# Four of the first 16 modulation pieces scaled by ScalarE and summed by TensorE, and the bias rows behind two loads

## The reference

```python
c_act = jax.nn.silu(c)
for l in range(DEPTH):
    mod = (c_act @ w_ada[l] + b_ada[l])[:, None, :]          # 1024 x 6144 weights
    sh_a, sc_a, g_a, sh_m, sc_m, g_m = jnp.split(mod, 6, axis=-1)
    h = x * (1.0 + sc_a) + sh_a
    proj = h @ w_in[l]
    ...      # three attention mixers, output projection w_o, layer norm
    ...      # second modulation, squared-ReLU MLP of width 4096, layer norm
```

## Time and profile before

| | us |
|---|---|
| median of 3 runs (lowest to highest) | 1343.76 (1343.13 to 1343.97) |
| the profiled execution, its own time | 1341.76 |
| its span (first to last instruction) | 1340.0 |
| TensorE busy in it | 1299.1 |
| VectorE busy in it | 972.2 |
| ScalarE busy in it | 603.3 |

### The profile page before, as it was taken

The page is one execution under the profiler, slowest core; times in us unless marked ns, Lnnn a source line. Parts: engine busy times, 40 slices in busy tenths (PEclk is TensorE's granted clock), DMA queues, the critical chain, the costliest instruction groups (busy, mean ns, idle before and its releaser), DMA issues.

```text
span 1340.0 us, 19979 instructions
## 1 busy us (share of the span) xinstructions
PE 1299.1 (97%) x6888; PEld 1106.5 (83%) x6888; DVE 972.2 (73%) x1646; ACT 603.3 (45%) x1244; POOL 317.2 (24%) x428
## 2 busy tenths in 40 slices
PE   7998999999999999999999999999999999999996
PEld 5897797988878888888879977888897888888885
DVE  6779898867787867876674668997679456544678
ACT  4465889824323222212255668995263222221321
POOL 0041376603010110010030506774130010001005
PEclk9999999999999999999999999999999999999998
DMA  9774100142644664462224330010335333323322
GB/s 360 282 233 143 57 1 28 64 154 68 234 159 158 224 206 146 172 225 88 85 69 151 113 122 1 15 46 24 118 124 181 97 95 97 100 94 95 101 94 102
DMA packets 89217, 165.09 MB, mean 123 GB/s; under 512 B 8435, under 2 KB 19059, under 8 KB 89132
## 3 DMA queue, kind: packets, MB, share of 16 engines
q1 hardware_dynamic: 88980, 163.71, 36.7%
q10 hardware_dynamic: 152, 0.28, 0.1%
HBM read 161.84 MB, written 4.21 MB: 124 GB/s over the span
## 4 chain that ended last, share of the span: by engine, by line
PE 77%; DVE 12%; ACT 5%; DMA 3%; POOL 1%; issue 1%; SPq 0%; DVEq 0%; ACTq 0%
PE bank L1790 23%; PE bank L1792 22%; PE bank L1791 22%; PE bank L2070 4%; DVE ada_sum L1091 2%; DMA ada_b<-in_b_ada 1%; PE bank L2054 1%; PE bank L1729 1%; DMA slab_raw<-in_w 1%; DVE stats L1453 1%; DVE sqr L1436 1%; PE bank L2046 1%; PE bank L2045 1%; DVE ada_sum L1118 1%; DVE h_lo L1540 1%
## 5 line engine op out<-in xcount | busy, mean ns | idle before, releaser
L1790 PE MATMUL bank<-hT_hi,slab_hi 128*128 128x512 f32 (+1 forms) x640 | 236.6, 370 | 3.0 <-DVE qC L1306 3.0
L1792 PE MATMUL bank<-hT_hi,slab_lo 128*128 128x512 f32 (+1 forms) x640 | 235.4, 368 | 0.0
L1791 PE MATMUL bank<-hT_lo,slab_hi 128*128 128x512 f32 (+1 forms) x640 | 235.4, 368 | 0.0
L1532 DVE TENSOR_TENSOR slab_lo<-slab_raw,slab_hi 128x512 fp32r<-128x512 f32 x240 | 166.7, 741 | 86.8 <-ACT slab_hi L1035 64.6
L1790 PE MATMUL bank<-slab_hi,h_hi 128*128 128x512 f32 x512 | 200.5, 392 | 1.9 <-DVE slab_lo L1532 1.9
L1792 PE MATMUL bank<-slab_hi,h_lo 128*128 128x512 f32 x512 | 199.3, 389 | 0.0
L1791 PE MATMUL bank<-slab_lo,h_hi 128*128 128x512 f32 x512 | 199.2, 389 | 0.0
L1790 PE MATMUL bank<-slab_hi,hT_hi 128*128 128x384 f32 (+3 forms) x448 | 154.2, 344 | 7.9 <-DVE slab_lo L1194 4.5
L1792 PE MATMUL bank<-slab_hi,hT_lo 128*128 128x384 f32 (+3 forms) x448 | 151.5, 338 | 0.0
L1791 PE MATMUL bank<-slab_lo,hT_hi 128*128 128x384 f32 (+3 forms) x448 | 151.5, 338 | 0.0
L1790 PEld LDWEIGHTS bank<-hT_hi,slab_hi 128*128 128x128 f32 x640 | 120.6, 188 | 25.3 <-DVE qC L1306 5.6
(11 more groups left out here) (224 smaller groups left out, 2453.5 us busy)
## 6 DMA issues: line engine op xcount, KB each, us to landing
slab_raw<-in_w SPq DMA_DIRECT2D x256, 256.0 KB, 2.8
ada_w<-in_w_ada SPq DMA_DIRECT2D x42, 1024.0 KB, 7.3
slab_raw<-in_w_in SPq DMA_DIRECT2D x48, 192.0 KB, 4.6
slab_raw<-in_w_o SPq DMA_DIRECT2D x32, 256.0 KB, 2.7
boot_w<-in_w_ada SPq DMA_DIRECT2D x6, 1024.0 KB, 11.8
slab_raw<-in_w_in SPq DMA_DIRECT2D x16, 256.0 KB, 2.7
band<-bias_rows SPq DMA_DIRECT2D x8, 448.0 KB, 4.4
slab_raw<-in_w_in SPq DMA_DIRECT2D x16, 144.0 KB, 2.1
```

Source lines behind the costliest of these rows:

```text
L1532: dve.tensor_tensor(slab_lo[:, slot, :], slab_raw[:, slot, :], f32(slab_hi[:, slot, :]), ALU.subtract).then_inc(slab_lo_done, 1)
L1790: pe.matmul(dst, a_hi, w_hi, start=first, stop=False)
L1791: pe.matmul(dst, a_hi, w_lo, start=False, stop=False)
L1792: return pe.matmul(dst, a_lo, w_hi, start=False, stop=last)
```

## The change

Four of the 16 pieces (3 and 7 of block 0, 6 and 7 of block 2) are no longer summed by VectorE. ScalarE scales each in place with `c_act`, and TensorE sums it over the partitions, 8 extra matmuls for a block, into a bank of its own; VectorE adds these columns to `boot_bias`, which `boot_mods` reads as before. The loads 0 and 1 go ahead of `rel_bias` and the one-hot table. TensorE starts with three `keep_busy` behind load 0, ahead of the table's matmuls, and has one more between the blocks. Transposes 2 and 3 use the banks of the shares, so they wait until these are read. ScalarE's copy and store of the bias rows move behind its first split.

```diff
+        SHARED = ((3, 7), (6, 7))
...
+            boot_load(0)
+            boot_load(1)
             sp.dma_start(rel[0:32, :], t_in["rel_bias"]).then_inc(rel_in, 16)
             sp.dma_start(onehot[:, :], t_in["onehot"]).then_inc(table_in, 16)
-            for n in range(4):
-                boot_load(n)
+            boot_load(2)
+            boot_load(3)
...
+            act.wait_ge(setup_dve, 1)
+            for b in range(2):
+                for k in SHARED[b]:
+                    n = 2 * b + k // 4
+                    w = boot_half(n)[:, k % 4, :]
+                    act.wait_ge(boot_in[n], 16)
+                    act.activation(w, w, ACT.Copy, scale=c_col[:, 1, k:k + 1]).then_inc(scaled, 1)
...
                 def boot():
+                    split(0, 384)
                     act.wait_ge(setup_pe, 1)
...
-                    split(0, 384)
                     act.wait_ge(boot_aff, 1)
...
             for b in range(2):
                 for k in range(KT):
-                    boot_piece(b, k)
+                    if k not in SHARED[b]:
+                        boot_piece(b, k)
             boot_split(0)
             dve.wait_ge(bias_in, 16)
+            for b in range(2):
+                dve.wait_ge(shares_done, b + 1)
+                cols = slice(8 * b, 8 * b + 4)
+                dve.tensor_tensor(boot_bias[:, cols], bank[2 + b][:, 0:4], boot_bias[:, cols], ALU.add
+                                  ).then_inc(bias_shared, 1)
+            dve.wait_ge(bias_shared, 2)
             boot_mods(0, bank[4][:, 0:4], bank[5][:, 0:4], boot_aff)
...
-                    pe.matmul(dst[:, :], ones[:, :], boot_half(1)[:, 0, :], start=True, stop=True)
+                    pe.matmul(dst[:, :], ones[:, :], boot_half(0)[:, 0, :], start=True, stop=True)
+            def shares(b):
+                pe.wait_ge(scaled, 2 * b + 2)
+                for c in range(4):
+                    for k in SHARED[b]:
+                        ins = pe.matmul(bank[2 + b][:, c:c + 1],
+                                        boot_half(2 * b + k // 4)[:, k % 4, P * c:P * c + P], ones[:, 0:1],
+                                        start=k == SHARED[b][0], stop=k == 7)
+                ins.then_inc(shares_done, 1)
+            pe.wait_ge(boot_in[0], 16)
+            keep_busy(bank[0], 3)
             pe.wait_ge(rel_in, 16)
             pe.wait_ge(table_in, 16)
...
-            pe.wait_ge(boot_in[1], 16)
-            keep_busy(bank[3], 5)
+            shares(0)
             pe.wait_ge(ada_half, 2)
             mod_cols(bank[4], ada_sum[:, 0, :])
+            keep_busy(bank[0], 1)
+            shares(1)
             pe.wait_ge(ada_half, 4)
             mod_cols(bank[5], ada_sum[:, 1, :])
             pe.wait_ge(x_in[0], 16)
             for k in range(4):
+                if k >= 2:
+                    pe.wait_ge(bias_shared, k - 1)
                 turn(k, range(TT))
```

More of the change, by code:

```diff
@@ L296, in trunk @@
         boot_aff = sem("boot_aff")
+        scaled, shares_done, bias_shared = sem("scaled"), sem("shares_done"), sem("bias_shared")
         slab_in = [sem(f"slab_in{i}") for i in range(RING)]
@@ L1106, in boot_piece @@
                 n = 2 * b + k // 4
+                own = [i for i in range(4 * (k // 4), 4 * (k // 4) + 4) if b >= 2 or i not in SHARED[b]]
                 if k % 4 == 0:
@@ L1119, in boot_piece @@
                                                    op0=ALU.mult, op1=ALU.add)
-                if k % 4 == 3:
+                if k == own[-1]:
                     ins.then_inc(ada_half, 1)
```

## The result

The changed kernel takes 1346.02 us (median of 20 runs, 1343.12 to 1349.31) against 1343.08 for the one before (20 runs, 1340.51 to 1346.71): ratio 1.0021, interval 1.0013 to 1.0028. It is slower by about 2.9 us, where 1.9 us faster was forecast, and 0.2 us above the top of the stated range. The profiled execution took 1346.76, its span is 1345.0.

A forecast was written before the change was run, and what follows sets the result against it. VectorE bounds the start-up until 19.57, then TensorE's queue until the first product at 24.94. TensorE's re-priced queue starts it at 23.0, 1.9 us sooner, so 1343.76 - 1.9 = 1341.9; range 1340.2 to 1345.8.

The forecast's parts named there:

- Loads: Start-up loads 0 to 3: each taken to land 0.9 us sooner, at 6.5, 9.0, 11.6 and 14.2.
- the two ends named: Bounds on the start-up loads: 0.9 us sooner as taken, or possibly nothing for loads 2 and 3.
- VectorE: Start-up sums with four pieces less: `ada_half` full at 16.1 against 19.5, 3.4 us sooner, and no longer last.
- the scaled copies: ScalarE's four start-up copies: 0.6 us each, bounds 0.5 to 0.8, ending at 15.4 and costing nothing.
- The failed step: TensorE's start-up queue: first product at 23.0 against 24.94, 1.9 us sooner, mostly from no idle time and a kept clock.
- the forecast queue: TensorE's start-up order of work: `mod_cols` of block 2 ends at 20.2, last `keep_busy` at 22.8, first product at 23.0.
- The rival that came true: One-column products do not hold TensorE's start-up clock: first product at 29 to 31, 4 to 6 us later; chance 0.15.
- Its last sum: At the low start-up clock, 16 transposes at up to 0.25 each and a `keep_busy` take some 3.5 to 5 us.
- The row that it rested on: The table's four start-up passes, 3.57 us with no gap, left the clock low: passes at 9.99 still took 0.86.
- The clock rule: The 16 start-up transposes hold the clock, giving 1341.9; by the skill's page a low stretch near 20 us gives 1343.6.
- What is late next: Behind the first product, the 1.9 us gain passes on through `mod_cols` at 42.20, the load at 58.42 and 67.12.
- the forecast of 1341.9: Whole-kernel median: 1343.76 less the 1.9 us won at the first product; chance 0.38.

The follow-up runs named there:

- e6: The kernel before with two more `keep_busy` in TensorE's idle time between the two start-up `mod_cols`: 1342.53 us, ratio 0.9995.
- e1: The changed kernel with 128 columns instead of one in the shares and the two start-up `mod_cols`: 1340.85 us, ratio 0.9987.
- e8: The kernel before with loads 0 and 1 issued ahead of `rel_bias` and the one-hot table, nothing else: 1343.42 us, ratio 0.9997.
- e4: The changed kernel without the one `keep_busy` between `mod_cols` of block 0 and the second shares: 1344.76 us, ratio 1.0016.
- e2: The changed kernel with 128 columns in the shares alone, the two start-up `mod_cols` keeping one column: 1340.93 us, ratio 0.9986.
- e7: The changed kernel with 128 columns in the shares and start-up `mod_cols`, without the middle and last `keep_busy`: 1340.55 us, ratio 0.9982.
- e11: Second measurement of e7, the changed kernel with 128 columns and without the middle and last `keep_busy`: 1340.73 us, ratio 0.9987.
- e10: The changed kernel without shared pieces, with 128 columns in the start-up `mod_cols` and five middle `keep_busy` instead of one: 1342.30 us, ratio 0.9992.

## Why the prediction was wrong

- *Loads.* Load 0 landed at 6.51 (6.5 forecast), load 1 at 9.31 (9.0), load 2 at 12.20 (11.6), load 3 at 14.73 (14.2). Loads 2 and 3 moved by 0.3 to 0.4, not 0.9: between the two ends named.
- *VectorE.* 16.69, forecast 16.1; the 0.6 are load 2's. It was off the path, as said. The same holds for the scaled copies, 0.72 for each of the first two and 1.33 for the last two together, for 0.6 each taken and within the bounds.
- *The failed step* is the one for TensorE, "Most of this comes from TensorE having no idle 1.9 us and so keeping its clock". Idle time is one way to lose it, and in the profile of e6 that reasoning holds. But the queue that replaced it is made of the table's four-column passes and one-column products, and I priced them at the rate of the high clock without a row in which a long run of them had kept it. The clock fell at 13.9, and each entry behind it has nearly its doubled price: `mod_cols` 1.71 for 1.0, `keep_busy` 1.92 for 0.86, the second shares 3.20 for 2.0, transposes 3.36 for 1.75; the first shares, in which it fell, took 2.79 for 2.0. With 128 columns (e1), nothing else changed, the forecast queue came about, and the time was 1340.85, 2.3 below its own runs of the kernel before.
- *The rival that came true* was the one with a chance of 0.15: a fall near 14.5, through `shares(1)` and the second `mod_cols`. It gave 29 to 31 for the first product, 28.74 was measured; it gave 1348 to 1350 for the time, and the median of 1346.02 stayed below that. Its mechanism came true, then, and its size did not. Its price for a one-column pass, 0.25, was too high: 1.71 us for eight passes is 0.21. (Its last sum was off as well: 16 transposes at 0.25 and a `keep_busy` of 1.7 are 5.7 us, and not 5 at most; measured were 3.36 + 0.86.) The row that it rested on, the table's four passes that left the clock low, has 2.10 us of idle time behind it. e8 shows the same without a gap: the `keep_busy` right behind the table still has a pass every 0.86 until 17.0. It was the best evidence there was, and I gave it too little weight against the picture of a queue with no gap.
- *The clock rule.* The Trainium skill, "TensorE: Matmul & The Clock Gate", section "Part 4: PE-mode transpose", says that transposes do not count as busy in the way that matmuls do. The measurement decides against it here: in e4 the clock rose at 25.9, and TensorE had done nothing but transposes since 22.5, and in e1 they ran at the high clock with products behind them still at it. The weak work here was the one-column product, with the table's passes ahead of it, and it was not the transposes.
- *What is late next.* The 3.8 us passed on whole to 46.01 and 62.19, as the forecast had it for its 1.9.
- *The size of the result.* The two profiles differ by 5.0 us, 3.8 ahead of the first product and 1.2 behind it, and the medians by 2.9. The profile of the kernel before was one of its quicker executions (1341.76, median 1343.08), and that of the changed kernel lies above its median (1346.76, median 1346.02). The 20 runs of the changed kernel spread over 6.2 us and go with the clock: the five quickest have a mean granted clock of 0.990 or 0.991, and of the eight slowest seven have 0.987. As an estimate from these, 0.004 of 1345 us is 10.8 us at 0.50 in place of 1.00, worth 5.4 us. So how long TensorE stays low changes from one execution to the next. Also, the forecast of 1341.9 started from the median of three runs, 1343.76; over 20 runs it is 1343.08, which hides 0.7: against the kernel before, 1.9 us less was forecast and 2.9 more measured, 4.8 us apart.

## What to carry to other kernels

A gap-free TensorE is not enough to keep its clock, as 13.9 to 27.5 in the changed kernel shows: look at what the instructions move. Where a product needs only one column of its result, as in a sum over partitions, try 128 columns and read one. Here a pass then took 0.13 us instead of 0.12 at the high clock, and in all four profiles with wide shares (e1, e2, e7, e11) that clock held until the first product. Before work is given to an engine to relieve another, price its whole queue at both clocks, and weigh the row nearest in kind to the new instructions over the one nearest in place.

## What the runs showed of the hardware that was not expected

- Work without gaps is not all alike to the clock: it rose under full-width `keep_busy` (near 9.9 in e1, where its weight loads begin to come every 0.43 us and not every 0.86) and under transposes (at 25.9 in e4). It fell under one-column products behind the table's 33-row, four-column ones (at 13.9 in the changed kernel, at 15.6 in e4), and the table's passes left it low in e8, where `keep_busy` followed at 0.86 a pass with no gap between.
- By the timelines eight one-column passes take 1.84 us at the low clock and 0.95 at the high one, 0.23 and 0.12 each, though each moves a single column. The weight loads beside them run nearly all that time (in e4 1.86 of 1.95 us for the first shares, at the high clock, and 3.53 of 3.55 for the second, at the low one), so the price seems to be that of the weights, and it goes with the clock too.
- Profiled executions differ behind the start-up as well. From the first product to the end of the span it was 1314.9 us in e7, with one low stretch in it ahead of the last one, and 1315.1 to 1319.2 in the others, which have two to four. It also matters where a stretch lies. The six profiles with none that starts between 65 and 76 have 1314.9 to 1316.2, the seven with one 1316.1 to 1319.2. A difference of 2 us between two single executions can thus be the clock's, as between e10 and e11, and at this size only medians over many runs are to be trusted.
